# Three raw slots in the output stage, three late adaLN loads, and expert loads asked for one by one

## What is computed

```python
mod = silu(cvec) @ w_ada + b_ada            # six rows of D: shift, scale, gate (1 and 2)
h = rmsnorm(x, g1) * (1 + scale1) + shift1
u_f, q, k, v, g_a, g_b = split(h @ w_in + b_in)
a = fourier_mix(u_f) @ w_fourier            # branch A
b = attention(q, k, v) @ w_na_o             # branch B
x = x + gate1 * ((sigmoid(g_a) * a + sigmoid(g_b) * b) @ w_out)
h2 = rmsnorm(x, g2) * (1 + scale2) + shift2
x = x + gate2 * moe(h2)                     # top-1 of 4 groups, top-2 of its 4 experts
y = rmsnorm(x, g_final)
```

## Time and profile before

| | us |
|---|---|
| median of the runs shown | 1196.16 |
| profiled execution | 1196.65 |
| its span | 1194.8 |
| TensorE busy in the span | 1116.9 |
| VectorE / ScalarE busy | 535.9 / 366.3 |
| start of iteration 80, by its first matmul | 609.1 |
| end of the last `w_out` load's matmuls | about 703.9 |
| first gather of tokens | 715.9 |

### The profile page before, as it was taken

How to read it: one execution, slowest core, us unless ns; L and a number is a source line. 1 busy time by engine, 2 the same in 40 slices (tenths; PEclk the granted TensorE clock), 3 DMA queues, 4 the chain that set the end, 5 groups by cost and what they waited for, 6 DMA issues and landing times.

```text
span 1194.8 us, 14481 instructions
## 1 busy us (share of the span) xinstructions
PE 1116.9 (93%) x5577; PEld 682.5 (57%) x5577; DVE 535.9 (45%) x781; ACT 366.3 (31%) x526; POOL 54.8 (5%) x100
## 2 busy tenths in 40 slices
PE   5899999999999999999999999999999888988795
PEld 2566766777777677667788875434344234423231
DVE  0464575555455444454466755242416041504056
ACT  3342342444433333333345533320112001201023
POOL 0210200110000220000010100000000000000000
PEclk9999999999999999999999999999999999999997
DMA  9999978887877898888898799999999999999994
GB/s 357 385 386 381 364 286 320 312 302 281 286 289 283 306 351 323 326 299 319 329 362 260 219 381 423 390 415 423 423 423 423 423 422 424 422 423 423 423 406 174
DMA packets 114964, 423.22 MB, mean 354 GB/s; under 512 B 9088, under 2 KB 9264, under 8 KB 82640
## 3 DMA queue, kind: packets, MB, share of 16 engines
q1 hardware_dynamic: 101968, 389.57, 83.4%
q0 software_dynamic: 5424, 15.35, 4.8%
q10 hardware_dynamic: 7504, 17.37, 4.0%
HBM read 418.27 MB, written 3.98 MB: 353 GB/s over the span
## 4 chain that ended last, share of the span: by engine, by line
PE 69%; DMA 27%; SPq 1%; DVE 1%; issue 1%; ACT 1%; DVEq 0%
PE bank L827 14%; PE bank L828 13%; PE bank L829 13%; PE bank L1196 10%; DMA mraw<-in_w_exp_up 10%; DMA mraw<-in_w_exp_down 5%; PE bank L808 5%; DMA raw<-in_w_in 4%; DMA mraw<-in_w_exp_gate 4%; PE bank L1235 3%; DMA raw<-in_w_ada 2%; PE bank L1135 2%; DMA mraw_y<-in_w_exp_gate 2%; PE bank L792 1%; PE bank L1277 1%; PE bank L1258 1%
## 5 line engine op out<-in xcount | busy, mean ns | idle before, releaser
L1724 DVE TENSOR_TENSOR w_lo<-raw,w_hi 128x1024 fp32r<-128x1024 f32 x192 | 231.8, 1223 | 246.7 <-ACT w_hi L1370 245.6
L1370 ACT ACTIVATE w_hi<-raw 128x1024 fp32r<-128x1024 f32 x192 | 200.3, 1057 | 313.3 <-DMA raw<-in_w_in 160.4
L827 PE MATMUL bank<-w_hi,h_hi 128*128 128x512 f32 x512 | 206.2, 403 | 6.6 <-DVE w_lo L1724 4.3
L828 PE MATMUL bank<-w_lo,h_hi 128*128 128x512 f32 x512 | 200.1, 391 | 0.0
L829 PE MATMUL bank<-w_hi,h_lo 128*128 128x512 f32 x512 | 199.8, 390 | 0.0
L1196 PE MATMUL bank<-mraw,xg 128*64 128x512 f32 x720 | 184.9, 597 | 12.5 <-DMA mraw<-in_w_exp_gate 4.8
L827 PEld LDWEIGHTS bank<-w_hi,h_hi 128*128 128x128 f32 x512 | 96.2, 188 | 47.1 <-issue 24.8
L1196 PEld LDWEIGHTS bank<-mraw,xg 128*64 128x64 f32 x720 | 57.7, 136 | 108.4 <-issue 105.6
L829 PEld LDWEIGHTS bank<-w_hi,h_lo 128*128 128x128 f32 x512 | 96.1, 188 | 21.0
L828 PEld LDWEIGHTS bank<-w_lo,h_hi 128*128 128x128 f32 x512 | 96.3, 188 | 18.1
L2190 DVE SCALAR_TENSOR_TENSOR d_lo<-bank,slot_w,d_hi 128x512 fp32r<-128x512 f32 x32 | 23.9, 747 | 161.6 <-ACT d_hi L1669 161.0
(11 more groups left out here) (293 smaller groups left out, 1332.2 us busy)
## 6 DMA issues: line engine op xcount, KB each, us to landing
raw<-in_w_in SPq DMA_DIRECT2D x64, 1024.0 KB, 8.3
raw<-in_w_ada SPq DMA_DIRECT2D x60, 1024.0 KB, 8.2
mraw<-in_w_exp_gate SPq DMA_DIRECT2D x46, 1024.0 KB, 20.8
mraw<-in_w_exp_up SPq DMA_DIRECT2D x44, 1024.0 KB, 20.9
mraw<-in_w_exp_down SPq DMA_DIRECT2D x42, 1024.0 KB, 20.6
araw<-in_w_ada SPq DMA_DIRECT2D x64, 512.0 KB, 10.9
raw<-in_w_out ACTq DMA_DIRECT2D x12, 1024.0 KB, 9.3
raw<-in_w_na_o SPq DMA_DIRECT2D x8, 1024.0 KB, 7.2
```

Source lines behind the costliest of these rows:

```text
L827: nc.tensor.matmul(o, hi[:, k, s], wh, start=k == first, stop=False)
L828: nc.tensor.matmul(o, hi[:, k, s], wl, start=False, stop=False)
L1370: nc.scalar.activation(w_hi[:, u % AHEAD], r, ACT.Copy).then_inc(hi_ready, 1)
L1724: v.tensor_tensor(w_lo[:, u % AHEAD], r, w_hi[:, u % AHEAD].bitcast(F32), ALU.subtract).then_inc(raw_done[n % RAW], 4)
```

## The change

1. LATE_ADA is 3. Ada load 92 has its place in the ring between dense loads 78 and 79, and TensorE does its `ada_super` alone behind the first unit of iteration 78. Behind the router super 93 stands before the ranking matmuls, 94 and 95 behind them as before.
2. From dense load 80 on (RING_CUT) the ring goes through slots 0, 1, 2 alone. Slot and turn come from a table. SP_DENSE and the iterations in which ScalarE asks for loads are unchanged: in iteration l it asks for load l + 4, whose slot is now that of load l + 1.
3. With slot 3 free since super 92, expert load 7 (its place lies over that slot) is asked for in the output stage. SyncE asks for 9 at `unit_used` >= 172 (iteration 86), 10 at 174, 8 at 178, 7 at 184 (iteration 92), then goes on as before.
4. Slot 0 now ends with super 94, slot 1 with 95, slot 2 with 93; load 4 waits for the first, 5 and 6 for the others. Before, slots 0 to 3 ended with 92, 93, 94 and 95.

```diff
-        LATE_ADA = 4
+        LATE_ADA = 3
...
+        RING_CUT = DENSE_AT[L_OUT]
+        ring_slots = [n % RAW if n < RING_CUT else (n - RING_CUT + RING_CUT % RAW) % (RAW - 1) for n in range(RING_LOADS)]
+
+        def ring_slot(n):
+
+            return ring_slots[n]
+
+        def ring_turn(n):
+
+            return ring_slots[:n].count(ring_slots[n])
+
+        def slot_end(slot):
+
+            return 8 * ring_slots.count(slot)
...
-            if n >= RAW:
-                queue.wait_ge(raw_done[n % RAW], 8 * (n // RAW))
+            if ring_turn(n):
+                queue.wait_ge(raw_done[ring_slot(n)], 8 * ring_turn(n))
...
+                sp.wait_ge(unit_used, 2 * L_OUT + 12)
                 first_gate_up_load(9)
+                sp.wait_ge(unit_used, 2 * L_OUT + 14)
                 first_gate_up_load(10)
                 sp.wait_ge(chunk_read, reads(21))
+                sp.wait_ge(unit_used, 2 * L_OUT + 18)
                 first_gate_up_load(8)
+                sp.wait_ge(raw_done[RAW - 1], slot_end(RAW - 1))
+                sp.wait_ge(unit_used, 2 * L_OUT + 24)
+                first_gate_up_load(2 * RAW - 1)
                 sp.wait_ge(unit_used, 2 * L_ALL - 4)
                 first_gate_up_load(15)
                 for n in (0, 2, 1, 3):
                     sp.wait_ge(unit_used, 2 * L_ALL - 2 + n % 2 * 2)
                     first_gate_up_load(n)
                 first_gate_up_load(12)
-                sp.wait_ge(raw_done[0], 8 * (RING_LOADS // RAW))
+                sp.wait_ge(raw_done[0], slot_end(0))
                 first_gate_up_load(RAW)
                 sp.wait_ge(route_done, NS)
                 first_gate_up_load(13)
                 first_gate_up_load(14)
-                for n in range(1, RAW):
-                    sp.wait_ge(raw_done[n], 8 * (RING_LOADS // RAW))
+                for n in range(1, RAW - 1):
+                    sp.wait_ge(raw_done[n], slot_end(n))
                     first_gate_up_load(RAW + n)
...
-            for a in (92, 93):
-                ada_super(a)
+            ada_super(93)
             pe.wait_ge(chosen_ready, 1)
```

More of the change, by code:

```diff
@@ L358, in backbone_step @@
         RING_LOADS = len(ring_order)
+        RING_CUT = DENSE_AT[L_OUT]
[6 more added lines that the diff above has]
+            return 8 * ring_slots.count(slot)
         def landed_count(n):
-            return 16 * (n // RAW) + 16
+            return 16 * ring_turn(n) + 16
         def ada_landed_count(n):
@@ L482, in ada_super_load @@
             slot_released(queue, n)
-            queue.dma_start(raw[:, n % RAW].rearrange("p (a k) n -> p a (k n)", a=1),
-                            ada_v[:, k:k + 1, super_chunk * D:(super_chunk + 1) * D]).then_inc(raw_landed[n % RAW], 16)
+            queue.dma_start(raw[:, ring_slot(n)].rearrange("p (a k) n -> p a (k n)", a=1),
+                            ada_v[:, k:k + 1, super_chunk * D:(super_chunk + 1) * D]).then_inc(raw_landed[ring_slot(n)], 16)
         def dense_load(queue, l):
@@ L498, in dense_load @@
             slot_released(queue, n)
-            queue.dma_start(raw[:, n % RAW], view[:, LOAD_K * quad:LOAD_K * quad + LOAD_K, col:col + COL]
-                            ).then_inc(raw_landed[n % RAW], 16)
+            queue.dma_start(raw[:, ring_slot(n)], view[:, LOAD_K * quad:LOAD_K * quad + LOAD_K, col:col + COL]
+                            ).then_inc(raw_landed[ring_slot(n)], 16)
         block = ctx.enter_context(nc.Block())
@@ L805, in ada_super @@
                         pe.wait_ge(ada_evac, super_chunk - GATE1)
-                pe.wait_ge(raw_landed[n % RAW], landed_count(n))
+                pe.wait_ge(raw_landed[ring_slot(n)], landed_count(n))
                 for g in range(4):
-                    last = nc.tensor.matmul(bank[7][32 * g:32 * g + 32], cpad[:, k], raw[:, n % RAW, g],
+                    last = nc.tensor.matmul(bank[7][32 * g:32 * g + 32], cpad[:, k], raw[:, ring_slot(n), g],
                                             start=k == 0, stop=k == KD - 1)
-                last.then_inc(raw_done[n % RAW], 8)
+                last.then_inc(raw_done[ring_slot(n)], 8)
             def unit(l, half):
@@ L819, in unit @@
                           (o_hi, o_lo) if (chunk - 8) % 4 == 2 else (f_hi, f_lo))
-                pe.wait_ge(raw_done[n % RAW], 8 * (n // RAW) + 4 * half + 4)
+                pe.wait_ge(raw_done[ring_slot(n)], 8 * ring_turn(n) + 4 * half + 4)
                 for t in range(UNIT_K):
@@ L835, in last_load @@
                 n = DENSE_AT[l]
-                pe.wait_ge(raw_done[n % RAW], 8 * (n // RAW) + 8)
+                pe.wait_ge(raw_done[ring_slot(n)], 8 * ring_turn(n) + 8)
                 for s in range(NS):
@@ L1365, in high @@
                 if u % 2 == 0:
-                    act.wait_ge(raw_landed[n % RAW], landed_count(n))
+                    act.wait_ge(raw_landed[ring_slot(n)], landed_count(n))
                 if u >= AHEAD:
                     act.wait_ge(unit_used, u - AHEAD + 1)
-                r = raw[:, n % RAW, (u % 2) * UNIT_K:(u % 2) * UNIT_K + UNIT_K]
+                r = raw[:, ring_slot(n), (u % 2) * UNIT_K:(u % 2) * UNIT_K + UNIT_K]
                 nc.scalar.activation(w_hi[:, u % AHEAD], r, ACT.Copy).then_inc(hi_ready, 1)
@@ L1446, in super_done @@
                 n = ADA_AT[A_SUPER + KD * (super_chunk - GATE1) + KD - 1]
-                act.wait_ge(raw_done[n % RAW], 8 * (n // RAW) + 8)
+                act.wait_ge(raw_done[ring_slot(n)], 8 * ring_turn(n) + 8)
             def evac_mod_rows(super_chunk, n):
@@ L1722, in low @@
                 dve.wait_ge(hi_ready, u + 1)
-                r = raw[:, n % RAW, (u % 2) * UNIT_K:(u % 2) * UNIT_K + UNIT_K]
+                r = raw[:, ring_slot(n), (u % 2) * UNIT_K:(u % 2) * UNIT_K + UNIT_K]
                 v.tensor_tensor(w_lo[:, u % AHEAD], r, w_hi[:, u % AHEAD].bitcast(F32), ALU.subtract
-                                ).then_inc(raw_done[n % RAW], 4)
+                                ).then_inc(raw_done[ring_slot(n)], 4)
             def chained(ins):
@@ L2118, in _ @@
             n = ADA_AT[95]
-            dve.wait_ge(raw_done[n % RAW], 8 * (n // RAW) + 8)
+            dve.wait_ge(raw_done[ring_slot(n)], 8 * ring_turn(n) + 8)
             dve.wait_ge(bias2_row_in, 64)
```

## The result

The changed kernel takes 1199.84 us (median, 1198.61 to 1200.79) against 1195.95 us (1194.88 to 1196.65) for the kernel before, measured beside it: ratio 1.0030, 95% interval 1.0020 to 1.0041. It is slower by some 4 us, 0.3 us outside the range of 1193.0 to 1199.5. The profiled executions stand at 1200.79 and 1196.65, spans 1198.9 and 1194.8.

What follows compares the result with a forecast made beforehand. TensorE was taken as the bound up to about 780 us, then the DMA. Terms of +0.93 and -0.6 us, the rest 0, gave +0.35 on the median of 1196.16: 1196.5 us, range 1193.0 to 1199.5.

Steps and rivals of the forecast that it cites:

- The bound, and where the extra prefetch goes: TensorE sets the pace to about 780 us, then the DMA; earlier loads only widen the gap at 750 to 785.
- The faster rival: The DMA counts all the way, so loads fewer behind 690 give 1194.0 to 1191.5 us; chance 0.24.
- Super 92 into iteration 78, +0.93 us: Ahead of the output stage, one more super on TensorE with no idle time to hide it: +0.93 us.
- Super 92 away from behind the router, -0.6 us: Behind the router, one super less lets ranking, `pick` and first gather start sooner, limited by `chosen`: -0.6 us.
- The clock rival: Behind the router, TensorE's clock stays at the lower level and supers run slowly: 1197.7 to 1198.7 us; chance 0.14.
- Three slots, at no cost: From dense load 80 on, raw loads are requested 2.3 us later but still land in time: 0 us.
- The gap behind the router, at no cost: Behind the output stage, load 4 goes out 3.2 us later, a DMA gap of about 2 us: cost 0.

Runs made afterwards that it cites:

- the filler's: Kernel before plus four unused matmuls of a super's shape behind the first unit of iteration 78: 1197.58 us, ratio 1.0013.
- super 92 late: Changed kernel with super 92 done behind the router again and load 7 asked for last; three slots kept: 1196.92 us, ratio 0.9993.
- late 3 alone: Kernel before with only LATE_ADA = 3, so super 92 runs in iteration 78; four slots and SyncE's order kept: 1198.68 us, ratio 1.0015.
- the first experiment: The same run as super 92 late: changed kernel with super 92 back behind the router, 1196.92 us, ratio 0.9993.
- super 92 left out: Kernel before with the four matmuls of super 92 not done anywhere, its slot given free once its data lands: 1198.80 us, ratio 1.0015.
- load 6 first: Changed kernel with SyncE asking for expert loads 13, 14 and 6 ahead of 4 and 5: 1198.35 us, ratio 1.0009.
- supers 93 and 94 first: Changed kernel with supers 93 and 94 ahead of the ranking matmuls and 95 alone behind them: 1199.20 us, ratio 1.0021.

## Why the prediction was wrong

**The bound, and where the extra prefetch goes: right.** TensorE had no wait for a load between 609 and 830 in either kernel, and the loads that came sooner widened the gap at 750 to 785, from 2.9 to 4.4 us of transfer. Filling the gap at 715 by hand moved most of it behind 725. The faster rival fell by this. And the end did follow TensorE: from the first expert matmul to the end all fourteen traces take 474.4 to 476.6 us, though that matmul begins between 718.6 and 723.6. (The GB/s line stands at 423 from slice 28 only up to slice 37; the last two slices are 406 and 174.)

**Super 92 into iteration 78, +0.93 us: right, a little small.** 1.0 us in the first trace, 1.05 in the filler's, 1.1 between the means of all traces.

**Super 92 away from behind the router, -0.6 us: this step failed.** It was worked out from the one trace of the kernel before, in which the pair ran at 1.2 GHz for most of its 3.23 us and so stood in the way of the ranking. The first half of the step came true there: the ranking begins sooner. The second half, that `pick`, the gathers and all behind them move with the ranking as one chain, did not. In us from the first matmul of iteration 80:

| | ranking | `pick` matmuls | first expert matmul |
|---|---|---|---|
| before, both traces | 102.61 | 106.04 | 110.61, 110.63 |
| changed, first trace | 101.98 | 106.97 | 112.45 |
| changed, second | 101.66 | 106.61 | 111.22 |
| changed, third | 101.66 | 106.65 | 111.87 |
| super 92 late, no stretch | 101.66 | 104.99 | 109.58 |
| late 3 alone, no stretch | 101.66 | 105.01 | 109.59 |

In the first trace of the changed kernel 0.63 us are won at the ranking. Then the time from the start of the ranking matmuls to VectorE's first use of their result is 0.6 us longer at the lower clock (1.59 in place of 0.97), which gives the whole gain back: VectorE begins `pick` 104.64 us behind the first matmul of iteration 80, 104.65 before. Supers 94 and 95, twice as long, overrun `pick`, which puts its matmuls 0.93 us later than before, and the `pick` and gather matmuls at the lower clock add 0.91. That is +1.84 us where the sum had -0.6. Over the three traces the term is +0.6 to +1.8, mean +1.2. Without a stretch `chosen` is waited for anyway (0.60 us with both supers), so the term is 0. No trace shows a gain at the experts.

With 1.0 for iteration 78 that makes +2.2 on the distance that counts; the spans of the three traces (mean 1197.9) lie 2.7 over the two of before (1195.15). The clock rival had this mechanism, priced at +1.2 to +2.2 over the forecast, but it stood at a chance of 0.14 and at "if the clock stays"; its far end of 1198.7 is 1.1 us under the median too, and it left out the slow ranking matmuls. The rows had what was needed: the clock fell behind the router and came back only after 2.7 us of supers without a gap, and the change put a gap just there. I read the level of the clock as a fixed property of the stage, when it is one of the things that the edit can change. The Trainium skill says in TensorE: Matmul & The Clock Gate, Part 1, that activity releases the throttle. The traces agree in that every stretch ended while TensorE was at work without a wait. That the clock fell at 707.8 in the kernel before with TensorE busy all the time, on the router's matmuls, goes beyond that sentence.

**Three slots, at no cost: right.** TensorE never waited for raw in the output stage, and the first experiment, which keeps three slots, lies at 0.9993. ScalarE's waits came as told, with less to spare for it than for TensorE: its timeline in the changed kernel has a wait for a raw load, which the depth of `w_hi` took up.

```profile
658.66 1.06 ACT L1390 ACTIVATE w_hi<-raw 128x1024 fp32r<-128x1024 f32 x1 [1.83 <-DMA raw<-in_w_out]
```

The request for load 90 went out 2.4 us later in the iteration than the earlier row's 643.41, at 646.81 with iteration 86 itself 1 us later, and landed 11.7 us after at the most (the slowest raw load between 570 and 720), against the 14.9 that I bounded it by and the 18.1 at which TensorE would have noticed.

**The gap behind the router, at no cost: no cost shown, and not shown to be free.** Load 4 went out at 715.43, later than the 713.7 forecast, since the ranking matmuls and super 94 ran slowly. With the first expert matmul late by 2.8 us the DMA had room. Filling the gap changed the time by 1.4 us on the median at most, with overlapping intervals.

**What stays open.** The median moved by 3.9 us in the first measurement and by 3.4 in the second; 1.0 and 1.2 of it are shown with their lines. Measured each by itself, the two halves of the move add up to the whole: 1.6 us for a super's work in iteration 78 and 2.4 for super 92 left out, 4.0 on the medians. But "LATE_ADA = 3 alone", which holds both, costs 2.2; the intervals of some 1 us on either side allow either. How often a stretch comes in each kernel is not known: only traces show it, three of three in the changed kernel and two of two in the kernel before, but in the variants that share a tail with one of them it was there once in six (load 6 first) and absent five times. Nor is it known how long it can be in the kernel before. Nine of its 87 executions beside the experiments took 1199.25 to 1200.47 us at mean clocks of 0.989 to 0.991, as the changed kernel mostly does, and none of these was traced. So the change may lengthen the stretch, or make long ones more frequent. The 2.4 us of super 92 left out, more than the 1.2 of the traces, would be explained by either, and the mean clocks do not say which.

## What to carry to other kernels

Work that TensorE does in place of a wait for another engine is not always free to take away: if dense work follows, it can decide at which clock the next microseconds run. Before costing an edit near a wait of TensorE, read the granted clock in 1 us windows on both sides, take more than one profile, and price the stage at both levels. And where a ring of slots sets the pace, as it did here up to 780, a load that is fetched ahead is given back at the next full ring; it was TensorE, which frees the slots, that set the end.

## What the runs showed of the hardware

With the same work of TensorE behind the router, the stretch at 1.2 GHz is there in some executions and not in others: 110.61 and 110.63 us of distance with it (both traces of the kernel before), 109.58 to 109.71 without (three variants). In one program its length varies: 10.2, 6.8 and 6.8 us in the three traces of the changed kernel. The clock fell at 707.8 in the kernel before with TensorE busy on the router's matmuls (128x20), and at 711.4 in the third trace of the changed kernel, in a wait of 1.46 us; the same wait had no fall in two other traces. The trace with supers 93 and 94 first has the clock fall, come back and fall again within 10 us. Removing four matmuls (0.93 us) made the kernel slower by 2.4 us; with four of the same shape in that place in the changed kernel, the two supers behind them took 1.92 us in place of 3.64 in the one trace of it.
